# Hybrid decoder trunk on one core: the token mixer's tiles, its vector work and its last steps in another order

## The reference

```python
xa, ya, q, k, v, g, lr, c = split_cols(x @ w_in)
out_a = rglru_group(xa, ya, ...)        # conv of 4 taps, gates, a scan over time, times gelu(ya)
out_b = gla_group(q, k, v, g, lr, ...)  # 4 heads of linear attention in chunks of 64 tokens,
                                        # decays from lr, RMS norm per head, times silu(g)
out_c = conformer_conv_group(c, ...)    # a * sigmoid(gate), conv of 31 taps, group norm, silu
return jnp.concatenate([out_a, out_b, out_c], -1) @ w_out
```

## Time and profile before

| | |
|---|---|
| median of 3 runs | 2375.29 us (2372.38 to 2375.81) |
| span of the profiled execution | 2371.9 us, all 25826 instructions |
| busy | PE 2253.1, POOL 1029.9, DVE 1115.7, ACT 808.3 us |
| mean granted clock of TensorE | 0.973 |
| mixer of layer 0, from its third tile to the third output tile | 396.53 to 591.18 us |
| the same in layer 1 | 1573.37 to 1764.57 us |

### The profile page before, as it was taken

How to read it: one execution, slowest core, us unless ns; L and a number is a source line. 1 busy time by engine, 2 the same in 40 slices (tenths; PEclk the granted TensorE clock), 3 DMA queues, 4 the chain that set the end, 5 groups by cost and what they waited for, 6 DMA issues and landing times.

```text
span 2371.9 us, 25826 instructions
## 1 busy us (share of the span) xinstructions
PE 2253.1 (95%) x10624; PEld 1874.2 (79%) x10624; DVE 1115.7 (47%) x1123; ACT 808.3 (34%) x1094; POOL 1029.9 (43%) x430
## 2 busy tenths in 40 slices
PE   7999999968999899999999999999799999999997
PEld 6888888856778788888878888887568788888886
DVE  2433236886643633333344333359877355333334
ACT  2322225625353422222243222245345344222223
POOL 5444445413472544444354444453244625444442
PEclk9999999978999999999999999999789999999999
DMA  4323322210341233332233332222113412333321
GB/s 167 95 96 101 110 91 72 90 39 26 122 135 52 72 98 97 97 107 98 77 95 98 98 108 98 88 77 76 49 59 100 131 54 71 98 98 98 112 98 48
DMA packets 55718, 213.20 MB, mean 90 GB/s; under 512 B 6064, under 2 KB 8368, under 8 KB 55344
## 3 DMA queue, kind: packets, MB, share of 16 engines
q1 hardware_dynamic: 54304, 207.64, 27.3%
q10 hardware_dynamic: 1296, 3.90, 0.5%
HBM read 209.42 MB, written 2.10 MB: 89 GB/s over the span
## 4 chain that ended last, share of the span: by engine, by line
PE 82%; DVE 10%; ACT 3%; DVEq 2%; ACTq 1%; POOL 1%; issue 1%; DMA 0%; SPq 0%
PE psum L462 24%; PE psum L463 23%; PE psum L466 23%; DVE tmp L1516 4%; PE psum L594 1%; POOL w_lo L385 1%; PE psum L498 1%; DVE x L1407 1%; ACT x L1034 1%; PE psum L478 1%; ACT w_hi L996 1%; PE psum L439 1%; ACT act_hi L1049 1%; PE psum L792 1%; PE psum L440 1%
## 5 line engine op out<-in xcount | busy, mean ns | idle before, releaser
L385 POOL TENSOR_TENSOR w_lo<-raw,w_hi 128x1024 fp32r<-128x1024 f32 (+2 forms) x360 | 944.2, 2625 | 1285.2 <-ACT w_hi L996 1285.1
L996 ACT ACTIVATE w_hi<-raw 128x1024 fp32r<-128x1024 f32 (+2 forms) x360 | 405.3, 1126 | 1334.5 <-PE psum L466 1220.1
L462 PE MATMUL psum<-act_hi,w_hi 128*128 128x512 f32 x1836 | 726.8, 396 | 35.2 <-ACT w_hi L996 35.2
L463 PE MATMUL psum<-act_lo,w_hi 128*128 128x512 f32 x1836 | 722.7, 394 | 0.0
L466 PE MATMUL psum<-act_hi,w_lo 128*128 128x512 f32 x1836 | 453.9, 389 | 0.0
L462 PEld LDWEIGHTS psum<-act_hi,w_hi 128*128 128x128 f32 x1836 | 350.0, 191 | 113.6 <-issue 35.5
L463 PEld LDWEIGHTS psum<-act_lo,w_hi 128*128 128x128 f32 x1836 | 350.3, 191 | 73.6 <-issue 0.5
L466 PEld LDWEIGHTS psum<-act_hi,w_lo 128*128 128x128 f32 x1836 | 344.7, 188 | 72.1
L1432 DVE TENSOR_TENSOR work<-work,psum 128x512 f32<-128x512 f32 x88 | 60.5, 687 | 609.8 <-PE psum L466 561.9
L1437 DVE TENSOR_TENSOR h_lo<-work,h_hi 128x512 fp32r<-128x512 f32 x88 | 240.5, 2733 | 6.9 <-issue 0.4
L462 PE MATMUL psum<-h_hi,w_hi 128*128 128x512 f32 x616 | 239.6, 389 | 0.0
(11 more groups left out here) (240 smaller groups left out, 2318.3 us busy)
## 6 DMA issues: line engine op xcount, KB each, us to landing
raw<-w_in SPq DMA_DIRECT2D x176, 512.0 KB, 3.5
raw<-w_out SPq DMA_DIRECT2D x64, 704.0 KB, 4.0
raw<-w_mix SPq DMA_DIRECT2D x36, 512.0 KB, 3.5
raw<-w_kv SPq DMA_DIRECT2D x32, 512.0 KB, 3.5
raw<-w_mixout SPq DMA_DIRECT2D x16, 576.0 KB, 3.8
raw<-w_q SPq DMA_DIRECT2D x16, 512.0 KB, 3.6
raw<-w_o SPq DMA_DIRECT2D x16, 512.0 KB, 3.5
raw<-w_v SPq DMA_DIRECT2D x4, 768.0 KB, 4.2
```

The costliest lines, as they stand in the source:

```text
L385: nc.gpsimd.tensor_tensor(w_lo[:, n % SPLIT, 0:width], raw[:, n % RAW, 0:width], w_hi[:, n % SPLIT, 0:width].bitcast(F32), ALU.subtract).t ...
L462: nc.tensor.matmul(o, hi, b_hi, start=start and k == 0, stop=False)
L463: nc.tensor.matmul(o, hi, b_lo, start=False, stop=False)
L996: A(w_hi[:, n % SPLIT, 0:width], raw[:, n % RAW, 0:width], ACT.Copy).then_inc(w_hi_made, 1)
```

## The change

Four things are changed together, in both layers. (1) The column tiles are projected in another order, and each names the tile whose reader must have left its bank (`BANK_FREE`). The second `cg` and `ca` tiles come after `q`, `g` 0 comes before the keys and is copied raw, with its silu later. (2) DVE does 14 taps of the first channel tile, then the decays, then the recurrent scans, and goes on with taps between the other steps. (3) The running sums of the taps lie in PSUM banks 2 and 3 (`CONV_BANK`), and the last tap writes the SBUF tile. (4) The reciprocals on DVE and the square roots on ACT are replaced: ACT gives `r = Abs_reciprocal_sqrt(v + eps)` and `r*r`, and DVE works out `r * (3 - (v + eps) r^2) / 2`, one Newton step, in three instructions. Besides, each chunk's update is made by four matmuls of 64x96 (two of 64x192 before), which fill both halves of the partitions, so that DVE takes a state in two instructions of 128x96 (four of 64x96 before), and the updates go through four banks. In the last steps `centered(0)` stands before the last 15 taps, `ya` 0 and 1 come earlier, and `MIX_ORDER` puts the convolution tiles last.

```diff
-V_SLOT = 13
+V_SLOT = 12
+MIX_TILES = [("xa", 0, 0, None), ("xa", 1, 1, None), ("xa", 2, 0, ("xa", 0)),
+             ("cg", 0, 1, ("xa", 1)), ("ca", 0, 2, None), ("g", 0, 0, ("xa", 2)),
+             ("k", 0, 1, ("cg", 0)), ("k", 1, 0, ("g", 0)), ("q", 0, 1, ("k", 0)),
+             ("q", 1, 0, ("k", 1)), ("cg", 1, 1, ("q", 0)), ("ca", 1, 3, None),
+             ("g", 1, 0, ("q", 1)), ("g", 2, 1, ("cg", 1)), ("g", 3, 0, ("g", 1)),
+             ("ya", 0, 1, ("g", 2)), ("ya", 1, 0, ("g", 3)), ("ya", 2, 1, ("ya", 0))]
+MIX_ORDER = [("r", 0), ("r", 1), ("r", 2), ("h", 0), ("h", 1), ("h", 2), ("h", 3), ("c", 0),
+             ("c", 1)]
+CONV_BANK = (2, 3)
...
@@ PE @@
+                def update(n):
+                    pe.wait_ge(ktok_read, layer + 1)
+                    if n >= 4:
+                        pe.wait_ge(state_ready, layer * (NCHUNK - 1) + n - 3)
...
+                        for r in range(2):
+                            h = 2 * g + r
+                            last = nc.tensor.matmul(
+                                psum[r * CHUNK:(r + 1) * CHUNK, 4 + n % 4, g * DV:(g + 1) * DV],
+                                k_tok[r0:r0 + CHUNK, t, h * CHUNK:(h + 1) * CHUNK],
+                                v_tok[r0:r0 + CHUNK, t, h * DV:(h + 1) * DV],
+                                start=True, stop=True)
...
+                project("cg", 0)
+                project("ca", 0)
+                pe.wait_ge(vectors_loaded, layer * 32 + 32)
+                recurrent_gates(0)
+                recurrent_gates(1)
+                project("g", 0)
+                recurrent_gates(2)
+                project("k", 0)
+                linear_gates()
+                project("k", 1)
+                project("q", 0)
+                project("q", 1)
+                project("cg", 1)
+                project("ca", 1)
+                values()
+                project("g", 1)
+                turned_keys()
+                project("g", 2)
+                for n in range(4):
+                    update(n)
+                project("g", 3)
+                for n in range(4, NCHUNK - 1):
+                    update(n)
+                project("ya", 0)
                 scores(0)
                 scores(1)
+                project("ya", 1)
                 output(0)
                 scores(2)
                 output(1)
                 scores(3)
+                group_norm(0, CC, conv_done, gn_mean)
                 rms(0)
                 rms(1)
                 output(2)
                 output(3)
                 project("ya", 2)
+                group_norm(1, CC, conv_done, gn_mean)
+                group_norm(0, SQ, gn_squared, gn_var)
                 rms(2)
                 rms(3)
+                group_norm(1, SQ, gn_squared, gn_var)
...
@@ ACT @@
+                    A(RS[h % 2][0:DV, :], bank(4 + h % 2, DV), ACT.Abs_reciprocal_sqrt,
+                      bias=small[0:DV, 47:48])
+                    act.drain()
+                    A(OSQ[h][0:DV, :], RS[h % 2][0:DV, :], ACT.Square).then_inc(rms_root, 1)
...
                 for g in range(2):
                     act.wait_ge(gla_cum, layer * 2 + g + 1)
                     A(EB[g], CU[g], ACT.Exp, scale=1 / 16)
                     A(KI[g], CU[g], ACT.Exp, scale=-1 / 16)
+                    if g:
+                        A(QQ[1], read("q", 1), ACT.Copy).then_inc(evac, 1)
                     A(GP[g], GP[g], ACT.Exp, scale=1 / 16).then_inc(gla_exp, 1)
...
@@ DVE @@
+                    total = bank(CONV_BANK[t])
...
+                            V.tensor_scalar(total, u_pad[:, t, 0:SEQ], w, vec(V_DB + t),
+                                            ALU.mult, ALU.add)
+                        elif j < CONV_K - 1:
+                            V.scalar_tensor_tensor(total, u_pad[:, t, j:j + SEQ], w, total,
                                                    ALU.mult, ALU.add)
...
+                            V.scalar_tensor_tensor(CC[t], u_pad[:, t, j:j + SEQ], w, total,
+                                                   ALU.mult, ALU.add).then_inc(conv_done, 1)
...
+                    V.scalar_tensor_tensor(b, b, EPS, OSQ[h][0:DV, :], ALU.add, ALU.mult)
                     dve.drain()
+                    V.scalar_tensor_tensor(b, b, -3.0, RS[h % 2][0:DV, :], ALU.add, ALU.mult)
                     dve.drain()
+                    V.scalar_tensor_tensor(o, o, vec(V_NG, DV), b, ALU.mult, ALU.mult).then_inc(
+                        rms_used, 1)
+                    dve.drain()
+                    V.scalar_tensor_tensor(o, o, -0.5, GG[h][0:DV, :], ALU.mult,
+                                           ALU.mult).then_inc(head_mixed, 1)
...
+                gated_input(0)
+                taps(0, 0, 14)
+                for g in range(2):
+                    decays(g)
+                for t in range(AT):
+                    scanned(t)
+                taps(0, 14, 20)
+                for g in range(2):
+                    decayed(g)
+                gated_input(1)
+                taps(0, 20, CONV_K)
+                taps(1, 0, 10)
+                for n in range(NCHUNK - 1):
+                    next_state(n)
+                taps(1, 10, 16)
                 mask(0)
                 mask(1)
+                centered(0)
+                taps(1, 16, 20)
+                mask(2)
+                mask(3)
                 recurrent(0)
                 recurrent(1)
+                taps(1, 20, CONV_K)
                 head(0)
                 head(1)
+                centered(1)
                 recurrent(2)
+                grouped(0)
                 head(2)
                 head(3)
+                grouped(1)
```

More of the change, by code:

```diff
@@ L1200, in mixer @@
                 act.wait_ge(rg_scanned, layer * AT + AT)
                 gelu(0)
[L1202 to L1204 removed]
+                gelu(1)
                 read_o(0)
[L1206 to L1208 removed]
@@ L1215, in mixer @@
+                for k in range(3, 7):
+                    hi(k)
                 for t in range(CT):
```

313 lines of the change are left out of this document (137 added, 176 removed), and 3 rows, old and new, of the table MIX_TILES.

## The result

The changed kernel takes **2334.66 us** (median of 4 runs, 2332.76 to 2338.7) against 2375.55 for the kernel before (4 runs, 2372.38 to 2377.01): a ratio of 0.9834, interval 0.9818 to 0.985. That is 40.9 us less. The forecast was 2330 us. The profiled execution took 2338.7 us, the slowest of the four, with a span of 2336.9, which is 35.0 less than the span before; the forecast for the span was 2327.0.

The account below looks back on a forecast made before the run. PE, busy 95% of the span, bounds the kernel. Mixers of 194.65 and 191.20 us become 170.5 each, 44.9 less, taking the span from 2371.9 to 2327.0; the median stands 3.4 above, so 2330 us, range 2312 to 2348.

Parts of the forecast that it names:

- the stall: PE's 16.25 us wait for `w_hi` behind the values goes in each mixer, 32.5 us for both.
- The new wait: PE idle 4.8 us ahead of the RMS sums, to 526.5, waiting for DVE's mask 2.
- The updates: PE's 28 small matmuls per mixer at 0.25 us each, 1.0 per chunk; bounds 0.12 and 0.26 per matmul.
- The clock: PE's clock in the mixer's sum: 1.4 us added, from the 3.45 us difference of the two mixers before.
- Nothing outside the mixers changes: The span beyond the two mixers stays the same; all 44.9 us of gain lie inside them.
- Taps in PSUM: DVE's taps with their sums in PSUM cost 0.83 us each; bounds 0.77 and 1.26.
- the 28: Sign of being wrong: the mixer's last stretch after `ya` 2 taking over 28 us.
- mixers of 168 to 172: Sign for the forecast: each mixer, third tile to third output tile, takes 168 to 172 us.
- A: Rival: POOL's lock costs DVE another 10 us, PE waits 5.4 at the transposes; 2341 to 2344; chance 0.15.
- B: Rival: mixer's end shorter, clock at 1.0, no POOL meetings, updates 0.12; 12 us less, 2318; chance 0.12.
- C: Rival: ACT's late logarithm delays `gla_cum`, the stall moves; 10 us lateness leaves 6.5 per layer, 2343; chance 0.10.
- D: Rival: DVE's taps on PSUM dear; gain gone at 1.40 us each, 2392 at 1.6; chance 0.05.

## Why the prediction was right, and where its sum was off

**The direction and the stall: right.** PE reaches the transposes at 480.93 (forecast 480.6), the mean at 520.39 to 521.5 (forecast end 521.7) and the RMS sums at 526.34 (forecast 526.5). DVE's idle time before the decays is 11.5 (some 10 forecast), its scans end at 468.0 (466.8), and splits of POOL met five of its instructions there, with 2.67, 2.67, 3.27, 3.99 and 4.00 us. The new wait is 4.83 (4.8 forecast). The first 45 us behind the values come out right, though, by two errors that cancel, as follows.

**The updates: dearer in the sum than on the chip.** The forecast took 1.0 us a chunk, 7.0 per mixer, with a lower bound of 0.12 per matmul, 0.48 a chunk. The row shows 0.22 a chunk: below the bound. The step that failed is the price of a matmul of half the width taken from the old ones run one after another. The two heads of a pair go to different halves of the array's columns here, and successive chunks to different halves of its rows: sixteen took 0.94 by the length of their row, against 1.67 for eight wide ones. The Trainium skill, TensorE: Matmul & The Clock Gate, Part 3: Packing small matmuls — row/col tiling, describes that matmuls in different parts of the array run at the same time; the rows here fit it, and I had not used it. No run sets the same matmuls into one part of the array, so this reading is not shown. Against that stand a wait of 1.82 for DVE at the updates, which I had named as a sign that I am wrong, 1.77 us for the last three chunks, which go at the pace of DVE's states, and 1.8 us of low clock in `ya` 0.

**The clock: the mis-sized term.** The forecast gave it 1.4 us per mixer. In the trace of layer 0 the RMS sums take 3.5 us for 1.8, outputs 2 and 3 take 541.09 - 529.83 = 11.26 for 6.28, `ya` 2 takes 548.61 - 541.09 = 7.52 for 5.44: 8.8 us. These are PE's rows there:

```profile
526.34 3.70 PE L805 MATMUL psum<-tmp,consts 96*96 96x512 f32 x4 [4.83 <-DVE tmp L1597]
529.83 0.63 PE L781 MATMUL psum<-tmp 128*96 128x128 f32 x2
...
541.09 0.79 PE L466 MATMUL psum<-act_hi,w_hi 128*128 128x512 f32 x1
...
548.61 1.88 PE L796 MATMUL psum<-tmp,consts 128*128 128x512 f32 x4
```

So `ya` 2 ends 8.6 us after the 540.0 of the forecast, and the next tile starts 8.6 after its 564.6: the stretch between them has the length forecast. Its steps do not all match, and that part is luck: centering 1 ends 1.8 us behind `ya` 2 and not 4.3, but ACT then loads a second table (1.28, for the gelu of `ya` 2) that the forecast did not have. With the 2.4 us that the forecast held for clock and splits, and a start 0.3 later, that is the mixer of 176.33 instead of 170.5. In layer 1 the clock was low for longer: the mixer is 182.07, with PE busy 6 us more for the same 751 records. What failed is the reading of the pair of mixers before: their difference of 3.45 us was taken as the whole of the clock's room, while both had lost time to it. In layer 0 the kernel before ran most of its last output and of its last `ya` tile at 1.2 GHz, from the row below on, without a gap of PE before it. (Half of 3.45 is also 1.7, and the sum has 1.4.)

```profile
555.42 0.74 PE L786 MATMUL psum<-tmp 128*96 128x128 f32 x2
```

In the changed kernel's layer 1 the clock fell one output before the wait; these are the stretches of the first output and of the second:

```profile
1667.96:1671.09 3.13, 3.13 (x23) 2.35 (x22) 0.00 (x0) 1.65 (x2) 1.69 (x1) 1.00 0.00 0
1672.55:1678.10 5.55, 5.55 (x24) 4.09 (x23) 0.00 (x0) 0.00 (x0) 0.00 (x0) 0.50 0.00 0
```

**"Nothing outside the mixers changes": wrong, to our favour.** 7.5 us came from the stretches behind, 5.5 of it, by the estimate above, by a shorter low clock right behind the mixers. It made up for a part of the 17.4 us by which the mixers fell short of 44.9, and left the profiled span 9.9 above the forecast's. The median, 2334.66, is only 4.7 above 2330, and that closeness is in part luck. The forecast put the median 3.4 above the profiled span, as it was before; the profiled execution after was the slowest of its four, so the median lies 2.2 below its span. By medians the gain is 40.9 of the 45 forecast, by spans 35.0 of 44.9. The four runs of the changed kernel also go with the clock, from 2338.7 at 0.977 to 2332.76 and 2332.99 at 0.981 and 0.982.

**Taps in PSUM: right.** 0.82 each, with DVE busy for 125.0 us in either mixer. The 2.7 us per mixer that I had worked out from the price for PSUM in the Trainium skill, VectorE: DVE Perf Modes, section The TRN2 errata, do not show: ten taps in PSUM take 8.23, and the uncontended taps of the earlier trace rows had a pitch of 0.83. What POOL's splits do to taps in SBUF weighs more: without this edit the change loses 22 to 25 us. The end of DVE's last stretch was right too, `ya` 2 to the next tile is 24.6 us, inside the 28. The marks that failed are the wait at the updates and mixers of 168 to 172.

**The rivals.** A's lock did not bite harder: 12.6 us instead of 12.2 over five meetings, no wait at the transposes. The 2.4 us that the prediction names there as a meeting's cap is the length of a split of 1024 columns; the two meetings with splits of 1536 cost 3.3 each. B had cheaper updates right and the clock wrong. C and D fell: the stall did not move, and no tap cost 1.40. C's cause, a late logarithm, did not occur. But the kernel before with its decays first shows that a stall can move: with the decays moved and nothing else, it goes to the transposes, the place that A had named, and grows. The parts taken back one by one cost 22 to 25, 17 to 20, 17 to 20 and 5 to 8 us, which is more than the 40.9 us that all of them gave. So their worth doesn't add up.

**Open.** Why the clock falls in the outputs with no gap before it is not settled: the filled wait and the early mean show that it does, and the new order of the end, which has a tile between the small matmuls and differs in other ways too, has less of it. No run varied the small matmuls alone, and in layer 0 of the new order without the added taps the last two outputs ran at the high clock throughout (0.46 a pair). The other parts were only taken back from the changed kernel: the sums in PSUM or the replaced reciprocals in the kernel before, alone, were not run, and the order of the column tiles was never varied by itself. That the reciprocals' extra cost is clock in both layers is read from one profile.

## What to carry to other kernels

When a stall of PE goes, price what PE does next at both levels of its clock, from rows at either level: behind a wait of 4.8 us, and within a row of small matmuls too, the same work took up to twice as long. Put the accumulator of a long chain of DVE steps into PSUM if POOL works beside it, and look where DVE or PE stands idle before moving work: here an earlier mean, a new order of the mixer's end with a dense tile in the middle of PE's small matmuls, and 13 more taps in an idle gap of DVE gave 33 to 36 us beyond the 40.9 of the change. And test a part alone before crediting it: the decays ahead of the scans, alone, made the kernel before 0.56% slower.

## What was not expected of the hardware

- Sixteen fp32 matmuls of 64 rows by 64 columns of weights and 96 columns of data, in alternating halves of the array, took 0.94 us at 2.4 GHz; eight of 64 by 128 with 192 columns took 1.67.
- TensorE's granted clock fell from 2.4 to 1.2 GHz while the engine had no gap, within a row of outputs made of matmuls of 64 and 128 columns (pairs from 0.46 to 0.74 us), in some profiles and not in others. With the wait ahead of them filled by 21 matmuls of 512 columns it fell at 532; without, PE began at the low clock behind the wait, at 526.34.
- A gain of the clock outlasted the stretch that was changed: by the estimate above 5.5 us came back right behind the mixers, where the granted clock was 0.71 and 0.81 before and 1.00 after.
- A DVE tap whose sum lies in PSUM was never held up by a split of POOL: 116 of 116 took 0.754 to 0.759 us, while of the 120 taps on SBUF alone in the kernel before 14 took 2.7 to 3.8.
